# Another modulation tile goes to TensorE, its small products are cut in three, and half-tile sums move to other units

## The reference

```python
silu_c = jax.nn.silu(c)                                   # c is 1 x 2048
m_l = (silu_c @ ada_w[i] + ada_b[i]).reshape(bsz, 1, N_MOD, D_MODEL)   # ada_w is 2048 x 12288
n_l = modulate(rmsnorm(h_lat, norm_g[i, 0]), m_l[:, :, 0], m_l[:, :, 1])
# chunk_mlp_mix
z = jax.nn.gelu(n_l @ w_in)                               # w_in is 2048 x 8192
u, v = jnp.split(z, 2, axis=-1)
...                                                       # norm and mixing of v
y = (u * s) @ w_out
h_lat = h_lat + m_l[:, :, 2] * y
n_l = modulate(rmsnorm(h_lat, norm_g[i, 1]), m_l[:, :, 3], m_l[:, :, 4])
```

## Time and profile before

| | us |
|---|---|
| median of three runs | 2316.41 |
| lowest, highest | 2311.22, 2317.02 |
| the profiled execution's own time | 2314.73 |
| its span, first to last instruction | 2312.8 |
| TensorE busy | 2273.4 (98%) |
| VectorE busy | 1568.8 (68%) |
| ScalarE busy | 1135.5 (49%) |
| moved by DMA | 493.05 MB, 213 GB/s on average |

### The profile page before, as it was taken

How to read it: one execution, slowest core, us unless ns; L and a number is a source line. 1 busy time by engine, 2 the same in 40 slices (tenths; PEclk the granted TensorE clock), 3 DMA queues, 4 the chain that set the end, 5 groups by cost and what they waited for, 6 DMA issues and landing times.

```text
span 2312.8 us, 34482 instructions
## 1 busy us (share of the span) xinstructions
PE 2273.4 (98%) x13265; PEld 1987.5 (86%) x13265; DVE 1568.8 (68%) x2120; ACT 1135.5 (49%) x1700; POOL 103.1 (4%) x202
## 2 busy tenths in 40 slices
PE   6999999999999999999999999999999999999998
PEld 5788888888788888888888889999999999878987
DVE  6888777777788865666656767566566645655655
ACT  3355444444465543555445554444544444565544
POOL 0010100111100000000000001000000000100000
PEclk9899999999999999999999999999999999999999
DMA  9999788798867765555655565444444544544453
GB/s 368 387 378 400 236 284 265 243 332 314 304 221 249 251 198 193 182 182 185 197 181 198 186 197 168 151 155 139 142 148 144 164 149 161 169 135 125 139 183 127
DMA packets 230041, 493.05 MB, mean 213 GB/s; under 512 B 9682, under 2 KB 12520, under 8 KB 226824
## 3 DMA queue, kind: packets, MB, share of 16 engines
q1 hardware_dynamic: 210384, 432.05, 55.0%
q0 software_dynamic: 14272, 50.99, 6.6%
q10 hardware_dynamic: 5256, 8.20, 1.1%
HBM read 488.49 MB, written 2.10 MB: 212 GB/s over the span
## 4 chain that ended last, share of the span: by engine, by line
PE 85%; DVE 7%; DMA 5%; issue 2%; ACT 1%; SPq 0%; POOLq 0%; DVEq 0%; ACTq 0%
PE ps L1880 31%; PE ps L1927 22%; PE ps L1941 13%; PE ps L1943 7%; DMA ada<-in_ada_w 4%; PE ps L2417 4%; DVE acc L1195 2%; DVE wlo L1127 2%; PE ps L2240 1%; DVE acc L1136 1%; PE ps L2402 1%; PE ps L2259 1%; PE ps L2048 1%; DMA raw<-in_a_w_in 1%; PE ps L2386 1%
## 5 line engine op out<-in xcount | busy, mean ns | idle before, releaser
L1127 DVE TENSOR_TENSOR wlo<-raw,whi 128x1024 fp32r<-128x1024 f32 x720 | 872.6, 1222 | 501.7 <-ACT whi L580 500.2
L580 ACT ACTIVATE whi<-raw 128x1024 fp32r<-128x1024 f32 x720 | 756.5, 1057 | 807.7 <-PE ps L1880 393.4
L1941 PE MATMUL ps<-xt__59,whi 128*128 128x512 f32 x1408 | 498.4, 399 | 1.8 <-DVE h L1352 0.7
L1943 PE MATMUL ps<-xt__59,wlo 128*128 128x256 f32 x1408 | 395.4, 281 | 0.0
L1880 PE MATMUL ps<-whi,xt__59 128*128 128x512 f32 x1024 | 333.7, 403 | 7.0 <-DVE xt__59 L1269 7.0
L1941 PEld LDWEIGHTS ps<-xt__59,whi 128*128 128x128 f32 x1408 | 264.5, 188 | 69.2 <-DVE h L1352 2.2
L1927 PE MATMUL ps<-xmh__60,whi 128*128 128x272 f32 x1088 | 322.7, 297 | 0.6 <-DVE h L1352 0.3
L1927 PE MATMUL ps<-xmh__60,wlo 128*128 128x272 f32 x1088 | 314.9, 289 | 0.0
L1927 PE MATMUL ps<-xml__61,whi 128*128 128x272 f32 x1088 | 313.0, 288 | 0.0
L1943 PEld LDWEIGHTS ps<-xt__59,wlo 128*128 128x128 f32 x1408 | 266.0, 189 | 0.1
L1880 PEld LDWEIGHTS ps<-whi,xt__59 128*128 128x128 f32 x1024 | 198.3, 194 | 49.1 <-issue 7.4
(11 more groups left out here) (338 smaller groups left out, 3241.7 us busy)
## 6 DMA issues: line engine op xcount, KB each, us to landing
raw<-in_a_w_in SPq DMA_DIRECT2D x128, 1024.0 KB, 5.3
raw<-in_ffn_w_up SPq DMA_DIRECT2D x88, 1024.0 KB, 5.1
ada<-in_ada_w POOLq DMA_DIRECT2D x96, 512.0 KB, 4.7
raw<-in_a_w_out SPq DMA_DIRECT2D x48, 1024.0 KB, 5.9
raw<-in_ffn_w_down SPq DMA_DIRECT2D x44, 1024.0 KB, 5.1
mods<-in_ada_w SPq DMA_DIRECT2D x64, 512.0 KB, 11.0
raw<-in_b_w_in SPq DMA_DIRECT2D x32, 1024.0 KB, 5.5
ada<-in_ada_w SPq DMA_DIRECT2D x16, 1024.0 KB, 9.6
```

Of the source, the lines that this page charges most:

```text
L580: act.activation(whi[:, r % 4], raw[:, r // 2, r % 2], ACT.Copy).then_inc(hi_ready, 1)
L1127: dve.tensor_tensor(wlo[:, r % 4], raw[:, r // 2, r % 2], whi[:, r % 4].bitcast(F32), ALU.subtract).then_inc(lo_ready, 1)
L1941: pe.matmul(both, whi[:, r % 4, i, c * P:c * P + P], xt_[:, :, k * T:k * T + T], start=first and i == 0, stop=last and i == 1, skip_group_ ...
L1943: return pe.matmul(ps[:, bank + c, 0:T], wlo[:, r % 4, i, c * P:c * P + P], xth[:, k, :], start=False, stop=last and i == 1, skip_group_ch ...
```

## The change

Tile 2 of groups 1 to 3 goes to TensorE instead of tile 3, and VectorE sums tile 3 instead of tile 2. The 16 small products are cut into pieces of 6, 6 and 4, which stand after units 4, 5 and 6 of the group instead of all after unit 6; TensorE waits for the tile and for ScalarE's copies before the first piece, and counts the tile as used after the third. The third of the late low parts stands after tile 3 instead of after tile 2. Twelve or so of the half-tile sums in the output stage change their unit.

```diff
-PE_MOD = ((6,), (3,), (3,), (3,))
+PE_MOD = ((6,), (2,), (2,), (2,))
+COLUMN_AT = {4: (0, 3), 5: (3, 6), 6: (6, 8)}
...
-LATE_LO = (0, 1, 2, 4)
+LATE_LO = (0, 1, 3, 4)
...
-ADA4_AT = [(0, t) for t in (6, 8, 9, 10, 11, 13, 14)] + [(1, t) for t in (0, 1, 5, 6, 8, 9, 11, 12, 14, 15)]\
-    + [(2, t) for t in (0, 1, 5, 6, 7, 9, 10, 12, 13, 15)] + [(3, t) for t in (0, 1, 4, 5, 6)]
+ADA4_AT = [(0, t) for t in (6, 8, 9, 10, 11, 13, 14)] + [(1, t) for t in (0, 4, 5, 6, 8, 9, 10, 11, 12, 13, 14)]\
+    + [(2, t) for t in (0, 4, 5, 6, 8, 9, 10, 12, 13, 14)]\
+    + [(3, t) for t in (0, 4, 5, 6)]
...
-            def mod_column(g, d):
+            def mod_column(g, d, first=0, end=8):
 
                 bank, s = 6 + g % 2, PE_MOD[g].index(d)
-                pe.wait_ge(mod_loaded[mod_slot(g, d)], mod_landed(g, d))
-                for jb in range(8):
+                if first == 0:
+                    pe.wait_ge(mod_loaded[mod_slot(g, d)], mod_landed(g, d))
+                for jb in range(first, end):
...
-                mm.then_inc(mod_turned, 1)
+                if end == 8:
+                    mm.then_inc(mod_turned, 1)
...
-                    if u == S_UNITS * g + 6 and g < 3:
-                        pe.wait_ge(sem("part_copied"), 2 * (g + 1))
-                        mod_column(g + 1, 3)
+                    i = u - S_UNITS * g
+                    if i in COLUMN_AT and g < 3:
+                        if COLUMN_AT[i][0] == 0:
+                            pe.wait_ge(sem("part_copied"), 2 * (g + 1))
+                        mod_column(g + 1, 2, *COLUMN_AT[i])
```

## The result

The changed kernel takes 2331.96 us (median of 6 runs, 2328.35 to 2334.38) against 2315.57 us (6 runs) for the one before: a ratio of 1.0073, interval 1.006 to 1.0086, so 14 to 20 us slower. The forecast was 2330.5. The profiled execution has a span of 2327.8 us, 15.0 more than the 2312.8 of the execution that the rows of before are from. TensorE was busy 2272.7 us of it, as before (2273.4): the loss is idle time.

The account below looks back on a forecast made before the run. DMA throughput and VectorE's chain were taken to bound the modulation stage, which delays TensorE's long run. 14.6 (stage) + 0.5 (clock) = +15.1 us on 2314.73 gives 2329.8, with 2330.5 us predicted for the median; range 2321 to 2338.

Parts of the forecast that it names:

- The place of the wait: SyncE's queue, groups 1 to 3: its wait for TensorE moves from behind four slabs to in front of tile 7.
- The queue runs dry at 62.2: Group 1's loads: tile 6 lands at 62.2 us and nothing follows until 64.3, so the DMA engines run dry.
- X: In each round, the end of TensorE's third piece of small products, which frees tile 2's slot for tile 7.
- X1 = 64.3: Group 1: the third piece ends at 60.80 + 3.49 = 64.3 us, all products lying before that.
- From X to the next start, 13.1: Each round: slab 0 lands 7.77 us after the third piece ends; VectorE's steps follow, TensorE's group starts at X + 13.1.
- TensorE's own pace, 24.25 and 25.3: From a group's start to the end of its third piece: 24.25 us in group 1, 25.3 in group 2.
- The sum of the stage: Modulation stage: rounds of 37.3 to 38.4 us against 32.7; group 3 starts at 153.15 against 138.51, +14.6 us.
- The clock: TensorE's restarts before each group: half clock after idle time, taken as +0.5 us; up to 9 us worse, 1 better.
- rival 3: TensorE's units 5 to 7: the small pieces lower the clock, 16 us in all, 2346 us; chance 0.05.
- The covered waits: Groups' units: ScalarE's copies covered by 0.5 us; VectorE's 0.6 us wait for tile 3 hidden, cost 0.
- Half-tile places, 0 of 0 to +3: Output stage, 429 to 603 us: moved half-tile sums cost VectorE some lead; bounds 0 to +3 us, taken as 0.
- The total: Whole kernel: 14.6 + 0.5 = +15.1 us, predicted 2330.5 us, 0.6% over the median.

## Why the prediction was right

**The place of the wait** was right, and it is the whole loss: with the wait moved behind the slabs (ring of six) nothing is lost, with it in place and every other part of the change taken out (tile 2 in one run, old places) all of it is.

**The queue runs dry at 62.2**: tile 6 lands at about 62. But 62.2 was counted in landings, and the DMA engines are without work earlier than that: their share is 0.12 over 60 to 62, and 0.06 over 60.3 to 61.5. The sum went from X to a landing and doesn't use this time, so nothing in it changes.

**X1 = 64.3** was 65.16: 0.9 late. The half clock at the start of group 0 lasted until 44.6 instead of 43.2, which is 0.7 us, and the rest lies in the joints between pieces and units. The products themselves took a little less, 1.25 + 1.25 + 0.8 = 3.3 us, than the 3.49 assumed.

**From X to the next start, 13.1**: 14.1 (65.16 to 79.28), 13.4 (103.56 to 116.92) and 13.4 (142.72 to 156.10), 1.6 in sum over the forecast. The term that was too small is the one from issue to landing. Slab 0 was cast 8.9, 8.1 and 8.1 us after X, where I had 7.77. Part of it is there at tile 7 already: VectorE takes up its sums at 70.71, 5.55 us after X, where I had 5.06. The quiet rows that I took the price from are from a stretch in which a slab was issued about every 5 us, and here six transfers are issued within 5 us; that this makes the difference was not tested. The estimate from the Trainium skill's page "DMA: Bandwidth & Descriptors" (section "Anatomy of one DMA — SWDGE (gpsimd) path"), 6.8 us, lies further off; that page's figure is fitted for transfers issued by GpSimd, and SyncE issues these. The measurement decides.

**TensorE's own pace, 24.25 and 25.3**: 24.28 and 25.80. Right in group 1, 0.5 short in group 2.

**The sum of the stage** was +14.6 at the start of group 3, and it is +17.6: 0.9 + 1.6 + 0.5. This was mis-sized in the same direction three times.

**The clock.** The pieces keep it: full (2.4 GHz) from 44.6 to 71.8, past unit 7, where before 63.8 to 70.5 was at half. In the kernel with the run after unit 4 the half clock (1.2 GHz) moves with the run, to 59.4 to 66.3. So in these traces a run of small products of 3.5 us beside units was followed by the fall each time, and the pieces of 0.8 to 1.3 us never; rival 3 did not come. At the starts TensorE ran at half clock until 82.1, 123.0 and 160.6: 2.8, 6.1 and 4.5 us after the starts, 6.7 us of price against 6.2 before. The +0.5 for it was right. That it comes at every start is what the Trainium skill, "TensorE: Matmul & The Clock Gate", section "HAM oscillation — how this bites in real kernels", says of a TensorE that waits for DMAs in every round; the trace agrees three times out of three (what TensorE waits for here are VectorE's results, which wait for DMAs). Before, with waits of 1 to 2 us, the half clock came at each of the three starts too.

**The covered waits.** VectorE's third sums waited for tile 3 by 0.36 to 0.73 us a round (0.55 in the row above), without a trace in TensorE's starts. TensorE's first piece followed unit 4 without a gap, so ScalarE's copies were in time.

**Half-tile places, 0 of 0 to +3**: one stall of 0.8 us at 552 in the changed kernel, none of that kind where the places stood alone; the times show no loss. The bound was reckoned a little high: the run of seven sums in units 8 to 14 stands in pass 1 only, pass 2 has six of them. In the whole stage six units lose a sum and six others get one.

**The total** came out nearer than its parts. The stage lost 18.1 us, with the half clock at the last start in it, and the profiled execution is 15.0 longer: some 3 came back in the long run of TensorE, 2.4 of them in the part that is some 272 or some 275 us long by execution. The nearness of 2330.5 to 2331.96 is in part this luck. The medians differ by 16.4 us; how much of the remaining 1.7 is this scatter and how much a small gain by the places stays open.

## What to carry to other kernels

With a ring of buffers, ask not only who frees a slot and when, but which transfer wants that slot next and what stands behind it in the issuing queue: the same wait cost nothing behind four slabs and 5 to 6.5 us a round in front of them. (Its length changed with its place: 2.1 us in all behind the slabs, 35.2 in front of them.) Price it as a closed loop: the release waits for the engine, the engine for the data behind the release, so the delay is paid in every round and isn't made up. A look at the DMA share in stretches of 2 to 4 us finds it; engines that are busy during the hole hide it in every average.

## What the runs showed of the hardware

The pace of TensorE at the same granted clock (1.00) and without idle time differs between executions of one and the same kernel: 96 units of the first feed-forward part took 271.9 us in one and 274.5 in another, and over 13 profiles of all kernels 271.9 to 272.5 in seven and 274.5 to 274.9 in six. Both profiles of the kernel with three pieces on tile 3 hold 1440 matmul records over these units, so it is the pace that differs. Its cause wasn't found. A difference of up to 3 us between two single profiles can be this, and only where the traces part tells it from the change.

After an empty queue the transfers landed later than single ones do: in the changed kernel the halves of tile 7, issued from 65.16 us on, landed 4.0 and 5.1 us after their issue and the slab behind them 7.9 us after its own, against 5.1 us in the median for a slab in the quiet stretch (4.9 at least).
